# Depthwise convolution taps stacked on TensorE through shifted rows in DRAM, modulation chunks between projections, and 768-token products in two halves

## What is computed

```python
mod_l = jnp.split(sc @ w_mod[i] + b_mod[i], 6, axis=-1)     # and mod_c for the context
hl = modulate(rms_norm(xl, norm1_g[i]), mod_l[0], mod_l[1])
...
def conv_module(h, w_pw1, w_dw, b_dw, ln_g, ln_b, w_pw2):
    u = h @ w_pw1                                            # 1024 -> 2048
    a, gate = jnp.split(u, 2, axis=-1)
    u = a * jax.nn.sigmoid(gate)
    u = lax.conv_general_dilated(u, w_dw[:, None, :], ...,   # depthwise, 31 taps over time
                                 padding=[(15, 15)]) + b_dw
    u = jax.nn.silu(layer_norm(u, ln_g, ln_b))
    return u @ w_pw2
...
xl = xl + mod_l[5] * (jnp.square(jax.nn.relu(h @ w_ff1[i])) @ w_ff2[i])
```

## Time and profile before

| | |
|---|---|
| median of 3 runs | 2348.62 us (2343.87 to 2348.84) |
| profiled execution | 2348.4 us, span 2346.1 us |
| mean granted TensorE clock | 0.974 of 2.4 GHz |
| PE busy | 2223.6 us (95%) |
| DVE, ACT, POOL busy | 1417.1 (60%), 807.3 (34%), 667.5 (28%) us |
| DMA | 312.12 MB, mean 133 GB/s |

### The profile page before, as it was taken

How to read it: one execution, slowest core, us unless ns; L and a number is a source line. 1 busy time by engine, 2 the same in 40 slices (tenths; PEclk the granted TensorE clock), 3 DMA queues, 4 the chain that set the end, 5 groups by cost and what they waited for, 6 DMA issues and landing times.

```text
span 2346.1 us, 30707 instructions
## 1 busy us (share of the span) xinstructions
PE 2223.6 (95%) x11666; PEld 1787.7 (76%) x11666; DVE 1417.1 (60%) x1872; ACT 807.3 (34%) x1145; POOL 667.5 (28%) x377
## 2 busy tenths in 40 slices
PE   6999969899999999998999999999997999899997
PEld 5677748788888888885457888887886888788885
DVE  5789982654444445544563754655418552699997
ACT  3212134211111111333663311111322543677775
POOL 0000014233333333431444344444542234011001
PEclk8999979999999999999999999999999999899999
DMA  9455532432222222220002233333232234599996
GB/s 309 156 160 169 198 124 81 179 138 63 63 63 63 63 63 63 66 72 10 10 1 64 83 98 92 97 98 113 72 90 63 63 76 153 188 394 403 406 405 252
DMA packets 248208, 312.12 MB, mean 133 GB/s; under 512 B 13642, under 2 KB 199595, under 8 KB 235827
## 3 DMA queue, kind: packets, MB, share of 16 engines
q1 hardware_dynamic: 236764, 275.33, 34.8%
q0 software_dynamic: 6688, 25.69, 2.8%
q10 hardware_dynamic: 4663, 9.79, 1.1%
HBM read 286.13 MB, written 24.65 MB: 132 GB/s over the span
## 4 chain that ended last, share of the span: by engine, by line
PE 84%; DVE 10%; ACT 2%; POOL 1%; DMA 1%; issue 1%; DVEq 0%; POOLq 0%; SPq 0%; ACTq 0%
PE acc L609 48%; PE acc L3013 8%; PE pb L3031 4%; PE acc L2524 3%; PE acc L2735 2%; PE pa L2749 2%; PE pb L2470 2%; PE pb L2762 2%; PE acc L661 2%; PE acc L643 2%; PE acc L2588 1%; DVE csum L1748 1%; DVE hid_hi L1813 1%; PE acc L690 1%; PE pa L2410 1%
## 5 line engine op out<-in xcount | busy, mean ns | idle before, releaser
L548 POOL TENSOR_TENSOR wlo<-raw,whi 128x1024 fp32r<-128x1024 f32 x180 | 449.5, 2498 | 907.1 <-ACT whi L537 887.0
L537 ACT ACTIVATE whi<-raw 128x1024 fp32r<-128x1024 f32 x188 | 198.4, 1059 | 890.3 <-PE acc L609 836.1
L609 PE MATMUL acc<-ah,whi 128*128 128x256 f32 (+1 forms) x1256 | 393.7, 362 | 5.0 <-DVE sg L2008 2.6
L609 PE MATMUL acc<-al,whi 128*128 128x256 f32 (+1 forms) x1256 | 389.4, 359 | 0.0
L609 PE MATMUL acc<-ah,wlo 128*128 128x256 f32 (+1 forms) x1256 | 388.9, 358 | 0.0
L609 PEld LDWEIGHTS acc<-ah,whi 128*128 128x128 f32 x1256 | 235.6, 189 | 48.3 <-issue 8.9
L609 PEld LDWEIGHTS acc<-ah,wlo 128*128 128x128 f32 x1256 | 236.7, 188 | 36.8
L609 PEld LDWEIGHTS acc<-al,whi 128*128 128x128 f32 x1256 | 236.7, 188 | 36.1 <-issue 0.5
L1833 DVE SCALAR_TENSOR_TENSOR x<-acc,mod,x 128x512 f32<-128x512 f32 (+1 forms) x174 | 109.7, 658 | 232.2 <-PE acc L609 232.1
L1037 DVE TENSOR_TENSOR expert_lo<-expert_pair,expert_hi 128x1024 fp32r<-128x1024 f32 x192 | 224.5, 1219 | 14.5 <-ACT expert_hi L1032 14.5
L1032 ACT ACTIVATE expert_hi<-expert_pair 128x1024 fp32r<-128x1024 f32 x192 | 201.4, 1059 | 63.4 <-PE acc L3013 40.1
(11 more groups left out here) (501 smaller groups left out, 3684.4 us busy)
## 6 DMA issues: line engine op xcount, KB each, us to landing
raw<-in_w_ff SPq DMA_DIRECT2D x128, 512.0 KB, 4.0
mod_raw<-in_w_mod SPq DMA_DIRECT2D x80, 512.0 KB, 5.8
expert_pair<-in_expert_w_gate SPq DMA_DIRECT2D x32, 1024.0 KB, 8.0
expert_pair<-in_expert_w_up SPq DMA_DIRECT2D x32, 1024.0 KB, 7.7
expert_pair<-in_expert_w_down SPq DMA_DIRECT2D x32, 1024.0 KB, 7.3
raw<-in_w_in SPq DMA_DIRECT2D x30, 512.0 KB, 3.8
raw<-in_conv_w_pw SPq DMA_DIRECT2D x24, 512.0 KB, 8.8
expert_rows_dram<-zero_rows POOLq DMA_DIRECT2D x1, 12288.0 KB, 38.1
```

The lines of the kernel that those rows point to most:

```text
L537: e.eng.activation(whi[e.n["q"] % 2][:, :], raw[r][:, :], ACT.Copy).then_inc(S["hi_ready"], 1)
L548: e.eng.tensor_tensor(wlo[b][:, :], raw[e.n["g"] % RING][:, :], whi[b][:, :].bitcast(F32), ALU.subtract).then_inc(S["lo_ready"], 1)
L609: ins = e.eng.matmul(o, w, m, start=keys.index(key) == n, stop=len(keys) - 1 - keys[::-1].index(key) == n)
```

## The change

1. **Stacked taps.** A *block* is 4 neighbouring taps. The gated rows of tile i are stored to DRAM and loaded back four times by SP, each time one column later, so that partition 32n + c of `shifted[:, g]` holds channel 32g + c moved by n columns. The weights `tap_rows` (128 x 128 for a block, made by POOL) hold for group g a 128 x 32 matrix with the four taps of each channel. Four matmuls, one for each column group, then do 4 taps. `TAP_BLOCKS` gives 3 blocks (12 taps) to tiles 0 to 5, 4 to tile 6 and 6 to tile 7; DVE keeps 19, 15 and 7 taps. DVE adds PE's sum at the tap in `SUMS_AT` and gates the next tile at the one in `GATE_AT`. `conv_taps(i)` stands one tile later in PE's order, so it reads rows that were stored a tile ago.
2. **Low parts.** The low parts of slots 4 to 15 are made by POOL instead of DVE. ACT makes no diagonals.
3. **Order of the chunks.** The second chunk of a tile is computed between its two projections instead of before both; chunk 4 is turned before slot 2, chunk 5 is computed between slots 2 and 3.
4. **Halves.** Products over all 768 tokens use segments 0:384 and 384:768 (`HALVES`), written at columns 128:512 and 512:896 of the bank. The instructions that read the banks take the new offset.
5. **Constants.** 18 instead of 12 small loads on ACT's queue at the start, for the taps in the order that the stacked weights want.

```diff
-PE_TAPS = (0, 6, 6, 6, 6, 6, 6, 9)
+SHIFTS = 4
+TAP_BLOCKS = (3, 3, 3, 3, 3, 3, 4, 6)
+GATE_AT = (16, 10, 10, 10, 10, 10, 10)
+SUMS_AT = (18, 15, 15, 15, 15, 15, 13, 6)
...
+    HALVES = [(0, TOK // 2, 1), (TOK // 2, TOK, 0)]
+    def unit_at(segs):
+        return CTX if segs is LATENT else P
...
+        def stack_rows(i):
+            sp.wait_ge(S["glu_done"], i + 1)
+            if i:
+                sp.wait_ge(S["shifted_in"], 64 * i)
+            sp.dma_start(u_t.ap(), upb[i % 2][:, :]).then_inc(S["gated_out"], 16)
+            sp.wait_ge(S["gated_out"], 16 * (i + 1))
+            if i:
+                sp.wait_ge(S["conv_summed"], i)
+            width = wide + SHIFTS * (TAP_BLOCKS[i] - 1)
+            for n in range(SHIFTS):
+                sp.dma_start(shifted[32 * n:32 * n + 32, :, 0:width],
+                             bass.AP(u_t, by_vector(i) + n, [[u_rows, 32], [32 * u_rows, 4], [1, width]])
+                             ).then_inc(S["shifted_in"], 16)
...
         for i in range(KT):
-            for n in CHUNKS_OF_TILE[i]:
+            mod_load(e, CHUNKS_OF_TILE[i][0])
+            load_pw(4 + 2 * i)
+            load_pw(5 + 2 * i)
+            for n in CHUNKS_OF_TILE[i][1:3]:
                 mod_load(e, n)
-                if n == CHUNKS_OF_TILE[i][0]:
-                    load_pw(4 + 2 * i)
-                    load_pw(5 + 2 * i)
+            stack_rows(i)
+            for n in CHUNKS_OF_TILE[i][3:]:
+                mod_load(e, n)
...
+        def place_taps(i):
+            if i >= 2:
+                pool.wait_ge(S["conv_summed"], i - 1)
+            for j in range(TAP_BLOCKS[i]):
+                ins = pool.tensor_tensor(tap_rows[i % 2][:, j, :].rearrange("p (g c) -> p g c", g=4),
+                                         mod_pick[:, :].unsqueeze(1).to_broadcast([P, 4, 32]),
+                                         stacked_taps(by_vector(i) + SHIFTS * j, i).unsqueeze(2).to_broadcast([P, 4, 32]),
+                                         ALU.mult)
+            ins.then_inc(S["diag_ready"], 1)
...
         def conv_taps(i):
-            pe.wait_ge(S["glu_done"], i + 1)
-            pe.wait_ge(S["diag_ready"], i)
-            if i >= 2:
-                pe.wait_ge(S["conv_taken"], i - 1)
-            count = PE_TAPS[i]
-            for j in range(count):
-                t = TAPS - count + j
-                for c0, c1 in ((0, 512), (512, wide)):
-                    ins = pe.matmul(pbk[:, c0:c1], diag[:, j, :], upb[i % 2][:, t + c0:t + c1], start=j == 0,
-                                    stop=j == count - 1)
+            pe.wait_ge(S["shifted_in"], 64 * (i + 1))
+            pe.wait_ge(S["diag_ready"], i + 1)
+            if i:
+                pe.wait_ge(S["conv_taken"], i)
+            count = TAP_BLOCKS[i]
+            for c0, c1 in ((0, 512), (512, wide)):
+                for j in range(count):
+                    for g in range(4):
+                        part = slice(32 * g, 32 * g + 32)
+                        ins = pe.matmul(pbk[part, c0:c1], tap_rows[i % 2][:, j, part],
+                                        shifted[:, g, SHIFTS * j + c0:SHIFTS * j + c1], start=j == 0, stop=j == count - 1)
...
+        pair(HALVES, 0)
+        for i in range(KT - 1):
             first, second = CHUNKS_OF_TILE[i]
-            mod_chunk(first, pa[:, 0:512], after_product=i > 1)
-            conv_taps(i)
+            mod_chunk(first, pa[:, 0:512], after_product=True)
+            if i:
+                conv_taps(i - 1)
             pe.wait_ge(S["mod_added"], first)
             turn_mod(first, turned_at(i, first))
+            project(2 * i + 2)
             mod_chunk(second, pa[:, 0:512])
-            project(2 * i + 2)
+            project(2 * i + 3)
             turn_mod(second, turned_at(i, second))
-            project(2 * i + 3)
-        conv_taps(KT - 1)
+        conv_taps(KT - 2)
         pe.wait_ge(S["acc_free"], e.at("u", 2))
         for n in LAST_CHUNKS:
+            if n == LAST_CHUNKS[-1]:
+                conv_taps(KT - 1)
```

156 lines of the change are left out of this document (76 added, 80 removed).

## The result

The changed kernel takes 2326.43 us in the median of 4 runs (2321.9 to 2328.49), the kernel before, run beside it, 2348.73. The ratio is 0.9906 with a 95% interval of 0.9887 to 0.9925: faster by 22.3 us, where 30 were forecast (2318 us, with 2306 to 2332 as the forecast's own range). The span of the profiled execution went from 2346.1 to 2323.8 us.

A forecast was written before the change was run, and what follows sets the result against it. PE was taken to set the convolution's period, DVE following 1.9 us behind, and to bound the MLP. 2348.4 - 10.1 (before T_2) - 20.0 (five periods) - 0 (tail) - 0 (halves) = 2318 us, own range 2306 to 2332.

The forecast's parts named there:

- Halves: nothing: Products over 768 tokens: two matmuls of 384 columns cost the same 346.7 ns as 256 plus 512; 0, +-4 us.
- Stacked taps: Convolution on PE: four column groups overlap, a four-tap block costs 1.335 us, a middle tile's taps 4.0 us instead of 8.0.
- upper bound of 1.76: Convolution on PE: most a block costs in us, its 271-column piece taking as long as a 512-column one; adds 10 us.
- Start: Start of the convolution: chunk 5 moves ahead, T_1 becomes 92.7, the next stretch an ordinary period; 10.1 us gained before T_2.
- Period: "It fits ... Nothing waits.": Convolution tiles: new DMA traffic takes 6.3 us, 22.7 in all within a 26.8 us period, so nothing becomes late.
- DMA sets the period: Rival, convolution: 32-partition rows at half rate, 29.0 us of DMA a tile, six periods lose 2.2 each; 2337 us, chance 0.14.
- DVE: 21.9 us: Convolution: DVE has 21.9 us of work in a 26.8 us tile; half a us of waiting is paid from slack.
- taps of the other form keep their 0.955 us: Convolution on DVE: beside POOL's work only two TENSOR_SCALAR instructions a tile slow down; other taps stay at 0.955 us.
- Tail: nothing: From T_7 to the mean's end: DVE's gain becomes a wait for DMA, length stays 42 us; bounds -7 to +6.

The follow-up runs named there:

- chunk_order_alone: The kernel before with only the new places of the modulation chunks; 2340.72 us, ratio 0.9947 to the kernel before.
- tail_alone: The changed kernel with tile 7's store on ACT's queue, and its loads and PE's last six blocks right after chunk 19; 2323.27 us, ratio 0.9867.
- low_parts_on_dve: The changed kernel with the low parts of slots 4 to 15 on DVE again, behind the first two taps after the gate; 2327.27 us, ratio 0.9901.

## Why the prediction was right, and where not

- **Halves: nothing.** Right. 579 matmuls in 100 us before, after and with the old cut, so a matmul of 384 columns costs what the mean of 256 and 512 does. The fixed 13.3 ns a matmul is the same for all three.
- **Stacked taps.** Right: three blocks take 99.77 - 95.70 = 4.07 us, 1.357 a block against 1.335 forecast. Four column groups overlap 3.9-fold (5.34 / 1.357), as the chunk's row said, not 3.07-fold. The forecast's upper bound of 1.76 was set a little low: two pieces as long as the chunk's row shows them are 1.85.
- **Start.** Right: T_1 at 93.1 against 92.7, and the first stretch became an ordinary period. chunk_order_alone shows it by itself. That T_1 came within 0.4 us is in part luck: it was 94.5 in tail_alone, which has the same instructions ahead of it.
- **Period: "It fits ... Nothing waits."** This is the step that failed, and the rival "DMA sets the period" had the mechanism. The undisturbed period is 26.38 us, under the forecast 26.8, mostly since the new order also saves 0.3 us (30.48 against 30.78 in chunk_order_alone). Over six periods that is 2.5 us which no term had, and by luck it covers half of the 4.9 us of waits. The rows were priced at 0.32 MB a us. They move at 16 x 3164 bytes / 252 ns = 0.20, so 1.62 MB take 8.1 us (by the median; by the sum of all packets' times 7.6 us a tile, and 4.8 on every fourth partition), and with the store's 0.42 MB at 0.41 a us about 9.1, not 6.3. A tile then has some 25.5 us of DMA work in 26.4. That is less than a period, so DMA does not quite bound it, but pieces of every second first chunk come late: 1.3 to 1.9 us each, 4.9 in all (163.18 - 158.28). The rival's own price, 2.2 us in every period, was too high: its 12.6 us doubled the store too, which runs at full rate, and it doubled the cost at a rate that short packets pull down. Of the 8818 packets in the earlier trace rows half are 512-byte pieces of weights at 32 ns, 0.26 MB a us over 16 engines, where a 2048-byte packet (84 ns) has 0.39 and a full-rate row 0.40.
- **DVE: 21.9 us.** The term failed and cost nothing. Gate to gate it has 26.9 us of work (148.22 - 0.74 - 120.58). 4.2 of the missing 5.0 us are the four taps behind the gate (8.03 against 3.87); most of the rest is the first tap of a tile, a TENSOR_SCALAR of 2.23 us beside POOL's sum over channels, which the forecast had put at nothing because DVE had slack. The sentence that taps of the other form keep their 0.955 us had no row behind it: the earlier trace rows show one POOL sum beside a TENSOR_SCALAR, and no low part of POOL beside a tap. Beside one, a tap takes 2.8 to 3.2 us. The Trainium skill, "SBUF — State Buffer", section "Who interferes with whom", says that a DVE instruction with two SBUF inputs contends with a GpSimd instruction that reads SBUF, and that the one that comes second waits for the whole of the first. The rows above agree: each of the two taps ends 0.83 us after a low part. low_parts_on_dve takes the low parts away from beside the taps, and the time stays. But the forecast's 4 us of slack are gone: the changed kernel's gates at 175.03 and 229.72 have no idle time before them.
- **Tail: nothing.** The chain of the forecast is the one that the trace shows: store behind two early chunks, rows late, PE idle, granted clock at half, blocks of 10.7 us (about 11 were forecast). The size was off: store landed at T_7 + 17.1, not 16, and the rows 10.0 us later at T_7 + 27.1, not 7 later at 23. The half rate accounts for 2.2 us of that, since rows on every fourth partition came 7.8 us after their store (275.50 - 267.72). The tail is 45.2 us, not 42.
- **Behind the stage.** 1.4 us go around one norm, where the granted clock is lower. No term had it, and no run was made for it.

In sum the forecast's 30.0 us lose 0.4 at T_1, 2.4 to T_7, 2.9 in the tail and 1.4 behind it. That leaves 22.9, which is the distance of the traces in the MLP. The forecast named the right gains; its total was 8 us too low mostly because waits for DMA, in the periods and in the tail, were priced too low.

## What to carry to other kernels

Price a transfer by the duration of its own kind of packet and by where it lands, not by a queue's average: on this chip the same 3 KB row cost 252 ns into 32 neighbouring partitions and 125 ns into 32 partitions spread over all 128, and a slowest dimension of 4 left 12 of 16 engines idle. When a change trades compute for a round trip through DRAM, look at the one place where nothing hides it, here the last tile: putting its store and loads ahead of two weight transfers shortened the tail by 5.6 us in the traces (42.6 to 37.1), though the totals' intervals overlap. An engine may have 5 us a tile more work than forecast and cost nothing, so test which engine is waited for before mending it; and look at it again once the other wait is gone.
